# Two transfers on GpSimd's queue that form the first weight sum of a gate/up set, in place of a VectorE addition

## The reference

```
def ffn_half(x, g, wg, wu, wd):
    h = rmsnorm(x, g)
    return x + 0.5 * ((jax.nn.silu(h @ wg) * (h @ wu)) @ wd)

def layer(h, ...):
    h = ffn_half(h, n1, w1g, w1u, w1d)
    z = rmsnorm(h, nm) @ w_in[l]
    m, st = token_mix(z, ...)          # chunk MLP, sliding-window and latent attention
    h = h + m @ w_out
    h = ffn_half(h, n2, w2g, w2u, w2d)
```

## Time and profile before

| | |
|---|---|
| median of 3 runs | 2032.18 us (2031.95 to 2032.79) |
| span of the profiled execution, first to last instruction | 2030.9 us |
| what lies around the span, median less span | 1.3 us |
| TensorE matmuls busy | 2015.1 us, 99% |
| VectorE busy | 1669.0 us, 82% |
| ScalarE busy | 973.4 us, 48% |
| GpSimd busy | 356.0 us, 18% |
| HBM read | 170.14 MB |

### The profile page before, as it was taken

One profiled execution on the slowest core, in us unless ns is written; L12 is line 12 of the kernel. 1 busy time (PEld: TensorE's weight loads), 2 busy tenths in 40 slices (PEclk: granted clock), 3 DMA queues, 4 the chain that ended last, 5 costly groups with the idle time before them and its releaser, 6 DMA issues.

```text
span 2030.9 us, 40762 instructions
## 1 busy us (share of the span) xinstructions
PE 2015.1 (99%) x15326; PEld 1962.2 (97%) x15326; DVE 1669.0 (82%) x2459; ACT 973.4 (48%) x1772; POOL 356.0 (18%) x218
## 2 busy tenths in 40 slices
PE   9999999999999999999999999999999999999998
PEld 8999999999879999999999999999987899999998
DVE  7999998755667999998689999976467599999975
ACT  6544453354646444453364444434546464444533
POOL 1222200032111222200012222001321213222000
PEclk9999999999999999999999999999999999999999
DMA  4323232342122232322223322324221123232331
GB/s 135 104 83 103 84 93 85 88 111 67 35 55 84 84 103 83 103 86 86 79 85 103 103 83 82 113 79 114 74 69 45 50 76 104 85 101 80 95 98 66
DMA packets 235894, 175.39 MB, mean 86 GB/s; under 512 B 35200, under 2 KB 232064, under 8 KB 235776
## 3 DMA queue, kind: packets, MB, share of 16 engines
q1 hardware_dynamic: 233664, 171.68, 28.4%
q10 hardware_dynamic: 2112, 2.10, 0.3%
HBM read 170.14 MB, written 3.62 MB: 86 GB/s over the span
## 4 chain that ended last, share of the span: by engine, by line
PE 92%; DVE 4%; ACT 2%; issue 1%; DMA 0%; DVEq 0%; SPq 0%
PE pair L1515 43%; PE pair L1464 32%; PE pair L1687 9%; PE pair L1837 1%; PE pair L1557 1%; DVE t_parts L2187 1%; PE pair L1817 1%; PE pair L1828 1%; PE pair L1823 1%; PE pair L1860 1%; PE pair L1845 1%; PE pair L1655 1%; ACT square L943 1%; DVE t_parts L2470 0%; DMA x_tok<-in_x_sample_dram 0%
## 5 line engine op out<-in xcount | busy, mean ns | idle before, releaser
L1515 PE MATMUL pair<-t_parts,chunk_high 128*128 128x288 f32 x4480 | 893.7, 295 | 2.3 <-issue 1.7
L1515 PEld LDWEIGHTS pair<-t_parts,chunk_high 128*128 128x128 f32 x4480 | 718.7, 188 | 3.8 <-DVE chunk_low L2152 3.8
L1515 PE MATMUL pair<-t_parts,chunk_low 128*128 128x288 f32 x2240 | 661.1, 295 | 0.0
L1515 PEld LDWEIGHTS pair<-t_parts,chunk_low 128*128 128x128 f32 x2240 | 420.9, 188 | 0.0
L988 ACT ACTIVATE chunk_high<-chunk_sum 128x512 fp32r<-128x512 f32 x320 | 199.4, 631 | 380.2 <-DVE chunk_sum L2140 184.7
L885 POOL TENSOR_TENSOR chunk_low<-set_raw,chunk_high 128x512 fp32r<-128x512 f32 x160 | 229.9, 1446 | 719.0 <-ACT chunk_high L988 719.0
L879 POOL TENSOR_TENSOR w_low<-raw,w_high 128x1024 fp32r<-128x1024 f32 (+1 forms) x46 | 113.0, 2459 | 590.4 <-ACT w_high L936 590.4
L2152 DVE TENSOR_TENSOR chunk_low<-chunk_sum,chunk_high 128x512 fp32r<-128x512 f32 x320 | 207.1, 689 | 8.1 <-ACT chunk_high L988 0.5
L1464 PE MATMUL pair<-hidden_high,w_high 128*128 128x288 f32 x868 | 186.1, 296 | 0.0
L1464 PE MATMUL pair<-hidden_high,w_low 128*128 128x288 f32 x868 | 185.9, 296 | 0.0
L1464 PE MATMUL pair<-hidden_low,w_high 128*128 128x288 f32 x868 | 185.6, 295 | 0.0
(11 more groups left out here) (312 smaller groups left out, 3833.5 us busy)
## 6 DMA issues: line engine op xcount, KB each, us to landing
set_raw<-in_w_gate_dram SPq DMA_DIRECT2D x44, 1024.0 KB, 5.3
set_raw<-in_w_up_dram SPq DMA_DIRECT2D x43, 1024.0 KB, 5.3
raw<-in_w_down_dram SPq DMA_DIRECT2D x64, 448.0 KB, 3.6
down_raw<-in_w_down_dram SPq DMA_DIRECT2D x16, 1024.0 KB, 5.1
raw<-in_w_in_dram SPq DMA_DIRECT2D x20, 512.0 KB, 3.9
raw<-in_w_in_dram SPq DMA_DIRECT2D x16, 256.0 KB, 3.9
raw<-in_w_out_dram SPq DMA_DIRECT2D x8, 512.0 KB, 3.4
raw<-in_w_out_dram SPq DMA_DIRECT2D x16, 256.0 KB, 3.9
```

Of the source, the lines that this page charges most:

```text
L1515: mm = nc.tensor.matmul(out, c[:, j, p, :], tr[p // 2][:, seat(p), x, t, :], start=p == 0 and n == 0, stop=p == KP - 1 and n == 2)
```

## The change

GpSimd makes S1 of every block set of a stage but the first, 19 in a stage. For set q it waits until TensorE has done product S1 of q - 1 (`chunk_used`), issues a transfer of the quarter of the even row tiles from HBM straight into `cf[:, S1]` (256 KB, 128 partitions x 4 runs of 512 B), waits until it has landed (`term_in`), and issues a second one of the odd row tiles that adds onto it (`sum_in`). Each stands behind the two remainders of the same set in GpSimd's queue. VectorE drops its addition and, behind `first_sums`, waits for `sum_in` and raises `chunk_sum` itself.

```
--- before.py
+++ after.py
@@ -572,6 +572,7 @@
         set_in = [sem(f"set_in{b}") for b in range(2)]
         chunk_high, chunk_sum, chunk_used = sem("chunk_high"), sem("chunk_sum"), sem("chunk_used")
         low_by_dve, low_by_pool = sem("low_by_dve"), sem("low_by_pool")
+        term_in, sum_in = sem("first_sum_term_in"), sem("first_sum_in")
         left_made, out_made = sem("left_made"), sem("out_made")
         b12_high, b12_ready = sem("b12_high"), sem("b12_ready")
         t_even, t_odd, t_sum = sem("t_even"), sem("t_odd"), sem("t_sum")
@@ -905,12 +906,29 @@
                     src = set_raw[b][:, :, :, n * P:(n + 1) * P].rearrange("p q e c -> p e q c")
                     nc.gpsimd.tensor_tensor(out=cl[:, js], in0=src, in1=ch[:, js].bitcast(F32), op=ALU.subtract).then_inc(low_by_pool, 1)
 
+            def first_sum(layer, w, i, b):
+
+                q = set_number(layer, w, i, b)
+                cols = slice(i * 2 * P + P, (i + 1) * 2 * P) if isinstance(i, int) else bass.ds(i * (2 * P) + P, P)
+                src = a[(("w1_up", "w1_gate"), ("w2_up", "w2_gate"))[w][b]][layer].rearrange("(q e p) n -> p q e n", e=2, p=P)
+                n = q - 3 * plain_before(layer, w) - 3
+                pool.wait_ge(chunk_used, 7 * q - 4)
+                pool.sem_inc(waits_passed, 1)
+                nc.gpsimd.dma_start(cf[:, S1], src[:, :, 0, cols]).then_inc(term_in, 16)
+                pool.wait_ge(term_in, 16 * n + 16)
+                pool.sem_inc(waits_passed, 1)
+                nc.gpsimd.dma_start(cf[:, S1], src[:, :, 1, cols], accum_op=ALU.add).then_inc(sum_in, 16)
+
             def ffn(layer, w, d):
                 for b in range(2):
                     plain_lows(layer, w, b)
-                with pool.Fori(1, MP) as i:
+                chunk_lows(set_number(layer, w, 1, 0), 0)
+                chunk_lows(set_number(layer, w, 1, 1), 1)
+                first_sum(layer, w, 1, 1)
+                with pool.Fori(2, MP) as i:
                     for b in range(2):
                         chunk_lows(set_number(layer, w, i, b), b)
+                        first_sum(layer, w, i, b)
                 pool.wait_ge(low_ready, layer * SLOTS + (d + RAW + DOWN_SLOTS))
 
             for layer in range(DEPTH):
@@ -2242,9 +2260,6 @@
                         for k in DOWN_ORDER[:2]:
                             hidden_low(ph, k)
                         low_for_pool(layer, base_slot)
-                    else:
-                        done(S1)
-                        combine(q + 1, 1 - b, S1)
                     if finish:
                         tile_out(i - 1, 0)
                     if b == 1 and opens:
@@ -2255,6 +2270,8 @@
                         dve.wait_ge(out_made, 4 * q - 4)
                     first_sums(q, b)
                     if not last:
+                        dve.wait_ge(sum_in, 16 * (q + 1 - 3 * plain_before(layer, w) - 3) + 16)
+                        dve.sem_inc(chunk_sum, 1)
                         combine(q + 1, 1 - b, S2)
                         chunk_low(q + 1, 1 - b, S1)
                     if finish:
```

3 lines of the change are left out of this document (removed).

## The result

The change takes the kernel from 2032.07 us (median of 4 runs) to 2709.31 us (4 runs, 2707.61 to 2710.9): 1.333 times, 95% interval 1.3314 to 1.3346. The forecast was 2705. The profiled execution took 2709.9 us with a span of 2708.2, 677.3 more than before.

The account below looks back on a forecast made before the run. TensorE's matmuls, busy 99% of 2030.9 us, were taken to bound the kernel. Four stages of 19D - 12.4 with D = 9.5 gave 672 us on the 2032.18 median: 2705 us, range 2400 to 3000.

Parts of the forecast that it names:

- the likeliest case: Gate/up stages: D from 7.2 to 12 us, giving 2530 to 2895 us, chance 0.62.
- D: Time from a sum's first transfer issue to its second landing on GpSimd's queue, put at 9.5 us.
- The cap on the gain: Gate/up stages: whatever VectorE is spared, time can fall by about 4 us at most, 0.2%.
- The relay: Each sum's transfers start only after the former sum passed VectorE, ScalarE and GpSimd; pair 11.66 + 9.93 + 2D us.
- The rival in which GpSimd's remainders are not in the loop: Loop holds only VectorE's S2 to second sums, TensorE's product and D: 14.9 us per set, 2316 us; chance 0.04.
- The rival of short landings: GpSimd's queue as quick as the quickest row, adding free: D = 5.6, 2408 us; chance 0.13.
- that of long ones: Landing or adding time goes by each transfer's 512 pieces: D = 13, 2971 us; chance 0.15.
- D - 2.6: Cost of a stage's first wait: transfers start as product S1 ends, 2.6 us before S2 would have started.
- 9 x (21.59 + 19.0 - 22.32): Mid-stage: nine pairs between first and last wait, each 21.59 + 2D us against 22.32 before.
- where 3.2 was forecast: Stage end: TensorE takes up the work it has in hand, recovering 3.2 us.
- the rival of that name: TensorE at 1.2 GHz throughout adds 152 us, 2857; a fall for part of each set costs nothing; chance 0.04.
- What would show it: Signs in gate/up stages: 76 VectorE waits of some 10 us, pair 21.6 + 2D, VectorE eased some 76 us.

Follow-up runs that it names:

- no_sum: Kernel before, with 76 first sums left out and nothing in their place: 2032.08 us beside 2032.54.
- ahead: Changed kernel, with both transfers of a sum ahead of GpSimd's two remainders of the same set in its queue: 2408.66 us.
- one_term: Changed kernel, with the second (adding) transfer left out, order kept: 2301.42 us.
- silu_after: Changed kernel, with ScalarE making A12's high part ahead of the two silus in even sets: 2641.82 us.
- plain_second: Changed kernel, with the second transfer overwriting instead of adding, same bytes, order and waits: 2607.11 us.
- sp_term_first: Changed kernel, with SP issuing the first transfer ahead of the set load in its queue, GpSimd only the adding one behind its remainders: 2421.5 us.
- one_term_ahead: Changed kernel, with the adding transfer left out and the remaining one ahead of GpSimd's remainders: 2070.69 us.

## Why the prediction was right

The forecast, 2705 us, was 4 us off the measured 2709.31, and the likeliest case was the one that came. The mechanism, a loop through three engines that pays D once a set, is what the runs show. That the number came within 4 us is luck: three terms were off and cancelled, and the largest, D, rested on stand-ins.

**The cap on the gain** held. The 3.8 us of the earlier trace rows was an upper end; `no_sum` shows 0.

**The relay** held, by its own place in the trace and by `ahead`, `one_term` and `silu_after`. The leg behind an even set's wait measured 9.61 us (267.26 to 276.87; forecast 9.93), the one behind an odd set's 11.30 (forecast 11.66). Both are a little short because VectorE's own work was quicker: S2 of the first took 0.69 us where the earlier trace rows has 0.94, and the two scalings of the gate in the second 1.73 where it has 2.03. In the earlier trace rows GpSimd's remainder of 211.78 to 213.08 runs beside that S2, and after the change none does; that this is the reason was not tested. The rival in which GpSimd's remainders are not in the loop (2316 us) falls with `ahead`: taking them out is worth 301 us.

**D** was to be 9.5 and is 9.75 (276.87 to 286.62) and 8.96 (297.92 to 306.88), mean 9.36. Its parts came out in another way than forecast. The first transfer was put at 3.9 and the adding one at 5.3 us. From issue to issue the two legs take 4.74 and 3.97, and from the second issue to S2 5.01 and 4.99. The adding transfer was the dearer, as chosen, and its price can now be named (`plain_second`). But the 5.3 was no measure of it. The prediction calls the 1 MB row the nearest above 256 KB, and the earlier trace rows has two nearer, 288 KB at 2.8 us and 512 KB at 8.0. With either in place of 5.3 the same sum gives 2515 or 2910. So 5.3 was a choice between them that came out. The 0.3 added for the set load came out near: the first transfer of the leg in which a set load is under way takes 4.74 against 3.97, 0.4 on average. The landing rows of the change give the two kinds together:

```profile
chunk_sum<-in_w_gate_dram POOLq DMA_DIRECT2D x80, 256.0 KB, 4.4
chunk_sum<-in_w_up_dram POOLq DMA_DIRECT2D x72, 256.0 KB, 4.5
```

The rival of short landings (D = 5.6) and that of long ones (D = 13) both fall. The fit of the Trainium skill (DMA: Bandwidth & Descriptors, "Anatomy of one DMA"), 2.6 us for 256 KB, an estimate by that page, is under every one measured here: a plain transfer on GpSimd's queue landed in 3.3 to 4.1 us, and in 5.1 beside a set load.

**The ledger of a stage.** S2 at the first wait, the last wait, and the next stage's first S2, after:

```profile
68.80 0.69 DVE L2156 TENSOR_TENSOR chunk_sum<-chunk_sum,set_raw 128x512 f32<-128x512 f32 x1 [10.63 <-DVEq L2274]
...
425.98 0.69 DVE L2156 TENSOR_TENSOR chunk_sum<-chunk_sum,set_raw 128x512 f32<-128x512 f32 x1 [9.61 <-DVEq L2274]
...
830.80 0.69 DVE L2156 TENSOR_TENSOR chunk_sum<-chunk_sum,set_raw 128x512 f32<-128x512 f32 x1
```

and before:

```profile
58.64 1.06 DVE L2138 TENSOR_TENSOR chunk_sum<-chunk_sum,set_raw 128x512 f32<-128x512 f32 x1
...
257.13 1.12 DVE L2138 TENSOR_TENSOR chunk_sum<-chunk_sum,set_raw 128x512 f32<-128x512 f32 x1
...
662.37 0.69 DVE L2138 TENSOR_TENSOR chunk_sum<-chunk_sum,set_raw 128x512 f32<-128x512 f32 x1
```

The delay of S2 is 10.16 us at the first wait, 168.85 at the last, and 168.43 at the next stage. So:
- The first wait costs 10.2, where D - 2.6 = 6.9 was forecast. The step that failed is "the transfers start as product S1 ends": they stood behind remainders there too, and were issued at 58.94, which is 0.3 us after the S2 of before (58.64) and not 2.6 ahead of it. With D = 9.86 there that is the 10.2.
- The nine pairs cost 158.7, where 9 x (21.59 + 19.0 - 22.32) = 164.4 was forecast. The pair measured 39.69 in the mean where 40.59 was forecast: two legs short by 0.68 together, and D, twice, by 0.14. The pairs of before are 22.05 in the mean of the stage and not 22.32, which takes 2.4 us of this back.
- TensorE gives back 0.4 at the end, where 3.2 was forecast. The forecast took the last set at full speed, and TensorE begins it at half clock, after an idle stretch as in every set:

```profile
431.00:433.00 2.00, 2.00 (x10) 2.00 (x9) 2.00 (x4) 0.81 (x2) 0.00 (x0) 0.50 0.00 0
```

Together 168.4 for 168.1. From first S2 to first S2 (the last to the end) the four stages cost 168.4, 171.6, 167.8 and 169.6, in all the 677 of the spans. From a stage's last S2 to the next one's first it is 0.3 to 0.6 us less than before each time (404.82 beside 405.24 in the first), so nothing outside the gate/up stages became slower.

**The clock** fell, as the rival of that name said, and cost next to nothing in mid-stage, as its other half said. The granted clock was 0.50 for some 7 to 10 us in each of the two sets read, TensorE worked in 4 to 6 of them, and its matmuls' busy time rose by 169 us. In mid-stage that goes into time in which it would otherwise have stood idle. At the end of a stage it takes those 3 us of catching up, some 11 us in all (2.8 x 4, an estimate from the ledger, tested by no run). Where the loop is shorter it enters: part of the misses of `ahead` and `sp_term_first` is a product S1 at half speed. The rule of the Trainium skill (TensorE: Matmul & The Clock Gate, Part 1), that idling throttles the array and activity releases it, agrees with the windows above.

**What would show it** held but for one point: 76 waits of VectorE, 9.6 us each (forecast some 10); the pair at 21.59 + 2D = 40.3 (39.62); 39.86 MB; VectorE eased by 86.8 us (forecast some 76; the other 10 were not traced). TensorE was to wait for S1's remainder, 9 us. It waits for the `second_sums`, 6.7 us. Both stand behind the same wait of VectorE, the `second_sums` one to two us later. The forecast took the first of them, and the later one is what releases TensorE. The wait is also shorter because the work between two of them runs partly at half clock. Neither changes the sum, since the loop of the change doesn't pass through TensorE.

## What to carry to other kernels

Before a wait goes into an engine's queue, follow what that engine's next outputs release, through every queue, until the path comes back to the wait. If it does, and a turn of it is longer than that of the engine that bounds the kernel, its whole latency is paid once in each turn, however idle the engines on it are. Price that path by its links, and ask what stands ahead of each link in its own in-order queue. The same two transfers cost 677 us behind GpSimd's remainders, 377 ahead of them, and nothing measurable (72 of the 76 sums) with a landing place of their own and a set's time to land. And test first what the relief is worth by leaving the work out: here that takes a few lines, and shows that there was nothing to win.

## What the runs showed of the hardware

- A transfer that adds onto its destination costs 1.35 us more for 256 KB than one that writes, and holds GpSimd for 1.28 us at issue in place of 0.81. It goes in 528 packets where a plain one of the same shape goes in 80 (46208 in all in the changed kernel, 12160 in `plain_second`).
- A small transfer that starts with a large load on another queue pays for it: in `one_term_ahead` 5.1 us to landing where it leaves 1.0 us behind a 1 MB set load, 3.4 where it leaves 1.3 us ahead; in `ahead` 6.1 to 7.2 us from issue to the next issue where the two leave within 0.2 us, 3.9 to 4.8 where the load leaves 0.6 us or more behind. Transfers for which nobody waits cost nothing all the same (37.76 MB, +0.4 us, within the interval).
- The granted clock fell to 0.50 in the sets of the changed kernel that were read, and stayed there for 4 to 6 us after the matmuls had begun again. In `one_term_ahead`, with pairs of 23 us in place of 22, it did not fall (0.999 over the run).
